# Expert stage of a two-block model: a third set of first-layer buffers for the spare pairs, and the second layer two pairs behind the first

## The reference

```python
def _moe_ffn(h, router_w, router_b, w1, w3, w2, sw1, sw3, sw2):
    scores = jax.nn.sigmoid((h @ router_w).astype(f32))
    ...
    _, idx = lax.top_k(sel, TOP_K)
    wts = jnp.take_along_axis(scores, idx, axis=1)
    wts = wts / jnp.sum(wts, -1, keepdims=True) * ROUTED_SCALE
    ...
    def body(acc, blk):
        tok, wt, e = blk
        xb = h[tok]
        hid = jax.nn.silu(xb @ w1[e]) * (xb @ w3[e])
        return acc.at[tok].add(wt[:, None] * (hid @ w2[e]).astype(f32)), None
    ...
    shared = (jax.nn.silu(h @ sw1) * (h @ sw3)) @ sw2
    return routed.astype(h.dtype) + shared
```

## Time and profile before

| | |
|---|---|
| runs | 2021.16, 2029.53, 2037.06 us (median 2029.53) |
| profiled execution | 2027.24 us, of which the span 2025.1 us |
| mean granted TensorE clock | 0.954 of full speed |
| TensorE busy | 1870.4 us, 92% of the span |
| VectorE, ScalarE, GpSimd busy | 48%, 32%, 16% |
| moved by DMA | 456.76 MB, mean 226 GB/s over the span |

### The profile page before, as it was taken

One profiled execution on the slowest core, in us unless ns is written; L12 is line 12 of the kernel. 1 busy time (PEld: TensorE's weight loads), 2 busy tenths in 40 slices (PEclk: granted clock), 3 DMA queues, 4 the chain that ended last, 5 costly groups with the idle time before them and its releaser, 6 DMA issues.

```text
span 2025.1 us, 33529 instructions
## 1 busy us (share of the span) xinstructions
PE 1870.4 (92%) x14234; PEld 1342.9 (66%) x14234; DVE 979.9 (48%) x1446; ACT 647.1 (32%) x1012; POOL 331.1 (16%) x316
## 2 busy tenths in 40 slices
PE   7989998999997999899999789979999999999981
PEld 6878998989997999765756679874333333333320
DVE  5745555465664677746545754663222222222116
ACT  5544334444454433420033532421211111211110
POOL 2100000000000100012200024402233333333413
PEclk9989999999998999999888789979999999999996
DMA  8534555544443877446596000075999999999995
GB/s 278 189 105 157 187 186 186 164 146 147 150 143 119 298 249 249 148 148 186 170 338 231 1 14 4 3 296 184 397 371 369 375 372 369 365 377 378 373 400 201
DMA packets 199700, 456.76 MB, mean 226 GB/s; under 512 B 32982, under 2 KB 154326, under 8 KB 170000
## 3 DMA queue, kind: packets, MB, share of 16 engines
q1 hardware_dynamic: 157104, 377.18, 51.6%
q0 software_dynamic: 35712, 58.00, 8.5%
q10 hardware_dynamic: 6752, 19.67, 2.7%
HBM read 549.91 MB, written 52.43 MB: 297 GB/s over the span
## 4 chain that ended last, share of the span: by engine, by line
PE 83%; DVE 7%; DMA 4%; ACT 3%; issue 2%; POOL 1%; SPq 0%; ACTq 0%; POOLq 0%; DVEq 0%
PE psum L349 33%; PE psum L3467 15%; PE psum L3451 7%; PE psum L1570 7%; PE psum L1577 2%; PE psum L3393 2%; PE psum L2607 2%; DMA mem<-in_exp_w_dram 2%; DMA mem<-in_exp_w_dram,mem 1%; PE psum L2591 1%; ACT w_hi L405 1%; PE psum L3480 1%; DVE w_lo L410 1%; PE psum L3150 1%; PE psum L569 1%
## 5 line engine op out<-in xcount | busy, mean ns | idle before, releaser
L410 DVE TENSOR_TENSOR w_lo<-mem,w_hi 128x2048 fp32r<-128x2048 f32 x122 | 279.3, 2292 | 229.5 <-ACT w_hi L405 226.9
L349 PE MATMUL psum<-x_hi,w_hi 128*128 128x256 f32 x1216 | 349.3, 287 | 4.5 <-DVE x_lo L556 4.5
L3467 PE MATMUL psum<-mem 128*64 128x512 f32 x1536 | 344.0, 601 | 8.8 <-DMA mem<-in_exp_w_dram,mem 7.5
L349 PE MATMUL psum<-x_hi,w_lo 128*128 128x256 f32 x1216 | 344.3, 283 | 0.0
L349 PE MATMUL psum<-x_lo,w_hi 128*128 128x256 f32 x1216 | 343.4, 282 | 0.0
L405 ACT ACTIVATE w_hi<-mem 128x2048 fp32r<-128x2048 f32 x122 | 233.8, 1918 | 193.7 <-PE psum L349 190.5
L3467 PEld LDWEIGHTS psum<-mem 128*64 128x64 f32 x1536 | 106.9, 138 | 207.4 <-issue 194.8
L349 PEld LDWEIGHTS psum<-x_hi,w_hi 128*128 128x128 f32 x1216 | 233.6, 192 | 10.2 <-DVE w_lo L410 4.8
L349 PEld LDWEIGHTS psum<-x_lo,w_hi 128*128 128x128 f32 x1216 | 237.2, 195 | 0.7
L349 PEld LDWEIGHTS psum<-x_hi,w_lo 128*128 128x128 f32 x1216 | 236.2, 194 | 0.0
L3451 PE MATMUL psum<-mem 128*64 128x512 f32 x768 | 175.3, 598 | 1.2 <-DVE mem L3553 1.2
(11 more groups left out here) (512 smaller groups left out, 2858.5 us busy)
## 6 DMA issues: line engine op xcount, KB each, us to landing
mem<-in_exp_w_dram SPq DMA_DIRECT2D x192, 1024.0 KB, 10.1
mem<-in_dil_w_qkv_dram SPq DMA_DIRECT2D x36, 1024.0 KB, 5.3
mem<-in_ada_w_dram POOLq DMA_DIRECT2D x48, 512.0 KB, 4.7
mem<-in_ffn_w_gate_dram SPq DMA_DIRECT2D x22, 1024.0 KB, 5.6
mem<-in_ffn_w_up_dram SPq DMA_DIRECT2D x22, 1024.0 KB, 5.5
mem<-in_ffn_w_down_dram SPq DMA_DIRECT2D x22, 1024.0 KB, 4.7
mem<-in_w_in_dram SPq DMA_DIRECT2D x13, 1024.0 KB, 5.5
mem<-in_na_w_qkv_dram SPq DMA_DIRECT2D x12, 1024.0 KB, 8.6
```

Source lines behind the costliest of these rows:

```text
L349: ins = pe.matmul(out, lhs[a], rhs[b], start=start and k == 0, stop=stop and k == 2, **kw)
L410: dve.tensor_tensor(w_lo[n % SLOTS][:, 0, :], ring[:, n % SLOTS, :], w_hi_f[n % HI][:, 0, :], ALU.subtract).then_inc(S("w_split"), 1)
L3467: ins = pe.matmul(psum[r, up, :].rearrange("p (a n) -> p a n", a=2), xg[:, b % 2, c, x * P + 64 * e:x * P + 64 * e + 64], w_up[s][e][:, :, ...
```

## The change

There are four parts.

1. *A third set of first-layer buffers for spare pairs.* `spare_slot` is four more 1 MB regions, in places that earlier stages used: behind the identity matrix in a ring of old buffers, in the transposed activations `aT`, at `base_top`, and over the low halves `xr_lo` of the tokens. Spare pairs use this set; own pairs alternate between the two old ones by their own number. So own rows of pair n wait for the first layer of own pair n − 2, and a spare fetch waits for the spare pair before it, three places earlier. The second-layer slots stay as they were. The fourth region is read by the gather of batches 0 and 1, so at pair 2 the fetch into it waits for `x_gathered` 8 and is issued on its own. The shared expert's weights now come into regions 0 and 2, so that all four first-layer rows of own pair 1 are loaded at once.
2. *Where the spare pairs stand.* `SPARE_AT` puts spare 0 at pair 26 and spare 1 at pair 38; unused ones stand at 43 and 45.
3. *TensorE's order.* The hidden rows' transposes of pair k − 1 come right before the gather's transposes of pair k, and the second layer of pair k − 2 behind them; the last two pairs are written out. `hid_T` has two buffers. VectorE, ScalarE and GpSimd follow (`y_out` two pairs later, `y_put` one).
4. *Small moves.* The router's weights go to `gain_b`, the order of constants changes so that the ones needed here lie beside the identity, and the loads of the last norm's vectors move from before the stage to pair 46 on ScalarE.

```diff
+    SPARE_AT = [15, 14, 6, 13, 2, 12, 5, 11, 0, 10, 4, 9, 1, 8, 3, 7]
     for n in range(14):
-        PAIRS += [("own", 2 * n), ("own", 2 * n + 1), ("spare", 15 - n)]
-    PAIRS += [("own", 28), ("spare", 1), ("own", 29), ("spare", 0), ("own", 30), ("own", 31)]
+        PAIRS += [("own", 2 * n), ("own", 2 * n + 1), ("spare", SPARE_AT[n])]
+    PAIRS += [("own", 28), ("spare", SPARE_AT[14]), ("own", 29), ("spare", SPARE_AT[15]), ("own", 30), ("own", 31)]
...
+    UP_SET = [2 if kind == "spare" else n % 2 for kind, n in PAIRS]
+    UP_LEFT = [max([j for j in range(k) if UP_SET[j] == UP_SET[k]], default=-1) for k in range(len(PAIRS))]
...
+    spare_at = [names["ident"][0] + P + ring_at + SLOTS * SLOT, aT_at, base_top, rwkv_bottom + 2 * D]
...
-        for k, (kind, n) in enumerate(PAIRS + [("end", 0)]):
...
-            if kind == "own":
-                if k >= 2:
-                    sp.wait_ge(*at("mx_up", k - 1))
-                up_rows(k, n, range(2))
...
-            elif k >= 3 and PAIRS[k - 1][0] == "own":
-                sp.wait_ge(*at("mx_y", k - 2))
-                down_rows(k - 1, PAIRS[k - 1][1], range(2))
+        for k in range(len(PAIRS)):
+            if k in UP_LEFT and PAIRS[UP_LEFT.index(k)][0] == "own":
+                sp.wait_ge(*at("mx_up", k + 1))
+                up_rows(PAIRS[UP_LEFT.index(k)][1])
+            if k >= 2 and PAIRS[k][0] == "own":
+                sp.wait_ge(*at("mx_y", k - 1))
+                down_rows(k, PAIRS[k][1], range(2))
...
-        def fetch_up(k, n):
-            pool.wait_ge(*at("mx_up", k - 1))
+        def fetch_up(k, n, qs):
+            if k > 2:
+                pool.wait_ge(*at("mx_up", UP_LEFT[k] + 1))
+            else:
+                pool.wait_ge(*at("sh_up", 2))
+            for q in qs:
+                if k == 2 and q == 3:
+                    pool.wait_ge(*at("x_gathered", 8))
...
+            if 0 < k < last:
+                turned(k - 1)
             if b + 1 < BATCHES:
                 for u in range(2):
                     gather_pe(pe, b + 1, 2 * x + u)
-            if k:
-                down(k - 1)
...
+            if 2 <= k < last:
+                down(k - 2)
+            if k == last - 1:
+                turned(k)
+                down(k - 1)
```

More of the change, by code:

```diff
@@ L192, in constants @@
     names, parts, off = {}, [], 0
+    f = {k: f[k] for k in ["ident"] + [k for k in f if k not in EXPERT_CST] + EXPERT_CST[1:]}
     for k, v in f.items():
@@ L3357, in moe_pool @@
         for k, (kind, n) in enumerate(PAIRS):
-            if kind == "spare":
-                fetch_up(k, n)
-            if k > 2 and PAIRS[k - 1][0] == "spare":
-                fetch_down(k - 1, PAIRS[k - 1][1])
+            if k + 1 < len(PAIRS) and PAIRS[k + 1][0] == "spare":
+                fetch_up(k + 1, PAIRS[k + 1][1], range(4 if k > 1 else 3))
+            if k > 3 and PAIRS[k - 2][0] == "spare":
+                fetch_down(k - 2, PAIRS[k - 2][1])
             if k and k % 2 == 0 and k // 2 + 1 < BATCHES:
                 rows(k // 2 + 1)
-            if k - 3 >= PLAIN:
-                y_put(pool, k - 3)
-        y_put(pool, len(PAIRS) - 3)
+            if k == 2:
+                fetch_up(k, n, [3])
+            if k - 4 >= PLAIN:
+                y_put(pool, k - 4)
+        for k in range(len(PAIRS) - 4, len(PAIRS) - 2):
+            y_put(pool, k)
     def y_put(pool, k):
@@ L3450, in down, with turned @@
                         r = slice(64 * e, 64 * e + 64)
-                        ins = pe.matmul(psum[r, 4 + h, :], hid_T[:, f, r], w_down[s][e][:, f, 512 * h:512 * h + 512],
+                        ins = pe.matmul(psum[r, 4 + h, :], hid_T[s][:, f, r], w_down[s][e][:, f, 512 * h:512 * h + 512],
                                         start=f == 0, stop=f == 1)
             ins.then_inc(S("mx_y"), 1)
+        def turned(k):
+            pe.wait_ge(*at("mx_hid", k + 1))
+            after(pe, "hid_T", k)
+            if k == 0:
+                pe.wait_ge(*at("spare_rows", 3))
+            for f in range(2):
+                ins = pe.transpose(bank(1, P, f * P), hid_tok[:, f::2], ident)
+            ins.then_inc(S("hid_turned"), 1)
+        last = len(PAIRS) - 1
         for k in range(len(PAIRS)):
@@ L3543, in moe_dve, with hid_turned @@
             one_hot_dve(dve, k)
+        last = len(PAIRS) - 1
+        def hid_turned(k):
+            dve.wait_ge(*at("hid_turned", k + 1))
+            after(dve, "mx_y", k - 1)
+            dve.tensor_copy(hid_T[k % 2], bank(1, 256).rearrange("p (c j) -> p c j", c=2)).then_inc(S("hid_T"), 1)
         for k in range(len(PAIRS)):
             b, x = divmod(k, 2)
+            if 0 < k < last:
+                hid_turned(k - 1)
             dve.wait_ge(*at("mx_silu", k + 1))
@@ L3548, in moe_dve @@
             dve.tensor_tensor(hid_tok, sil, bank((0, 6)[k % 2], 256, 256), ALU.mult).then_inc(S("mx_hid"), 1)
-            if k:
+            if 2 <= k < last:
+                y_dve(dve, k - 2)
+            if k == last - 1:
+                hid_turned(k)
                 y_dve(dve, k - 1)
-            dve.wait_ge(*at("hid_turned", k + 1))
-            after(dve, "mx_y", k)
-            dve.tensor_copy(hid_T, bank(1, 256).rearrange("p (c j) -> p c j", c=2)).then_inc(S("hid_T"), 1)
             if k == 0:
@@ L3564, in moe_dve @@
                 gate_dve(dve, k - 2)
-        y_dve(dve, len(PAIRS) - 1)
+        y_dve(dve, last - 1)
+        hid_turned(last)
+        y_dve(dve, last)
         for r in range(3):
```

72 lines of the change are left out of this document (36 added, 36 removed).

## The result

The changed kernel takes 2042.85 us (median of 14 runs, 2034.68 to 2054.38) where the kernel before takes 2025.97 (14 runs, 2017.55 to 2037.06). The ratio is 1.0082, with a 95% interval of 1.0064 to 1.0101: it is 0.8% slower. The forecast was 11 us more and 2038, within 1% of before and on the slow side; by the medians 16.9 us more is what came.

What follows compares the result with a forecast made beforehand. TensorE was taken as the bound by a hair, DMA (95.7%) right behind. Terms −8.6 + 0 − 8.8 − 2.1 + 7.9 + 2.1 + 17 + 3 + 0.5 = +11.0 on 2027.24 gave 2038 us, range 2013 to 2053.

Steps and rivals of the forecast that it cites:

- TensorE's saving: Expert stage: moved hidden-row transposes save 0.36 us in each of about 24 pairs without slot sums, −8.6 us.
- The end: Positions 43 and 45: waits on rows vanish, −8.8 us, and the matmuls behind the long one run faster, −2.1.
- The wait at pair 2: First layer of pair 2 waits 7.9 us for a spare fetch issued after the gather, plus 2.1 of lowered clock.
- DMA: Used spares' 9.44 MB amid own rows: three or four second-layer waits after pairs 23, 26 and 35, +17 us.
- the balance: Estimate of the DMA term: total transfer time of 488.5 us against the 473 TensorE wants, 15.5 us short.
- the sharing: Estimate of the DMA term: spares' data takes about half the engines for 43.2 us, own rows 18.7 us late.
- head-room: Own rows' queue, per three pairs: 35.8 us of transfer against 35.9 us of TensorE, so no slack left.
- Lowered clock: TensorE's clock drops after waits: +2.1 us behind pair 2's wait, +3 behind one or two second-layer waits.
- The tail: End of the stage, paced by GpSimd: one more group of transposes ahead of pair 45's second layer, +0.5 us.
- steady-pace rival: Own rows' queue can't keep the new pace, so TensorE's gain returns as waits: 2048 or 2053 us; chance 0.19.
- absorbed: Rival: first-layer rows' extra lead takes up the spare data, no second layer waits: 2018 us; chance 0.22.

Runs made afterwards that it cites:

- the order alone: Changed kernel without the third set, spare pairs placed and fetched as before, only TensorE's order and what follows it kept: 2041.46 us, ratio 1.0080.
- the early gather: Changed kernel with batch 1's whole matmul gather behind pair 0 and pair 2's fourth fetch ahead of the token rows: 2032.83 us, ratio 1.0028.
- the last run: Changed kernel with the early gather, the swap on SyncE, spare 0 at pair 2 and spare 1 at pair 38: 2015.39 us, ratio 0.9945.
- the swap on SyncE: Changed kernel, second own pair of each three: its second-layer rows issued ahead of first-layer rows of the pair three further on: 2034.50 us, ratio 1.0027.

## Why the prediction was right, point by point

**TensorE's saving.** Forecast −8.6, found about −9.7. Two pairs together, one without slot sums and one with them, save 0.45 us (0.31 and 0.14), against 0.36 by the forecast. Its working for the pair without them comes out: 0.37, the 0.31 and 0.06 more in the first layer behind, 6.96 us (1454.28 to 1461.24) instead of 7.02. The slot sums alone cost 0.18 (1442.27 to 1442.45), not 0.28, so that one distance was too long. But the forecast counted this term as independent of DMA. The run with the order alone shows that it isn't: without the third set it is lost and more.

**The end.** Forecast −10.9, found: no wait on rows at pairs 43 and 45.

**The wait at pair 2.** Forecast 7.9 and 2.1 of clock; 8.15 and 1.6 came, and the early gather took both away. This step held in place, size and cause.

**DMA.** Forecast 17 us as second-layer waits shortly after pairs 23, 26 and 35; 20.0 us came, in pairs 24, 30 and 36 and small ones in 6 and 12. Place, form and the half-and-half share (51.7 to 49.1%) held, and leaving the data out gave 25 us with the clock. One wait was longer than the 2 to 8 us forecast for each, 9.95. The term was a little low: between the balance's 15.5 and the sharing's 18.7 I took 17, and the sharing was nearer; the small waits of 1.53 and 0.81 us are the head-room that was gone. The balance gave the small queues 1.4% where the trace of before has 1.1, which makes it 14 rather than 15.5. It took the engines as full all through; from 1440 us on they were, but for 15 us behind pair 2's wait they carried next to nothing, which no term of the forecast has. What the experiments bear out is the account of the queue and of the place of the data, not a lack of capacity over the whole stage. The figure of about 358 GB/s for transfers from HBM, from the Trainium skill (DMA: Bandwidth & Descriptors, Where 436 GB/s comes from), is further off than in the kernel before: the last run carries 387 over 460 us.

**Lowered clock.** Forecast 2.1 + 3, found 9.3. This is the largest miss. I gave the second-layer waits one or two drops; behind three of the five it dropped, and the drop behind the wait of 2.94 us cost more (2.98) than that behind 9.95 (2.18). The waits of 1.53 and 0.81 us cost nothing more.

**The rest.** The tail got 1.7 us shorter instead of 0.5 longer; why was not followed up. The forecast said that the second layer two pairs back needs nothing sooner; near the end, in pair 46, it waits 0.99 us for VectorE (L3574). The forecast's steady-pace rival, priced at 2048 and 2053, is what the order alone runs into, and the third set keeps it off; "absorbed" is what the swap on SyncE begins to bring about, and only with the early gather and the data moved as well does the kernel come out faster.

**The total.** That 2038 lies within 5 us of 2042.85 is in part luck. In the profile 3.0 us of waits, 4.2 of lowered clock and 1.0 for VectorE were missing in the sum, and 1.1 of TensorE's saving and 2.2 of the tail offset a part of them. And the sum was added to 2027.24, an execution that lies 1.3 us over the median of 14.

## What to carry to other kernels

When TensorE and DMA are both nearly full, a saving on one has to be priced with the other: ask what each queue will deliver by the new, earlier need, and which of its rows are wanted first. In one queue, rows issued first held up rows issued behind them (the swap was worth 8 to 9 us by the medians), so a larger buffer for rows wanted late can put them ahead of rows wanted soon; issue by need, not by the moment a buffer comes free. And a wait on TensorE has a second price in the lowered clock behind it: here 2 to 3 us for each of three waits of 2.94 to 9.95 us.

## What the runs showed that I had not expected

- The lowered clock behind a wait doesn't grow with the wait: 2.98 us behind 2.94, 2.48 behind 4.77, 2.18 behind 9.95; in the run with the swap nothing behind 2.40 us (pair 37's first layer took its usual 7.09), and in the run with the order alone 1.69 behind 2.35 (the same pair's took 8.78).
- The parts of a row don't land together: in the run without the spares' data the last of 32 landing marks came 2.54 us behind the one before it, and TensorE waited 2.85 us.
- A fetch that moves next to nothing can cost 8 us: that at pair 2 was issued at 1409.52 and released TensorE at 1416.91, in a stretch in which own rows filled the engines (their queue at 100.5% from 1409 to 1417).
